# Who multiplies the attention probabilities: VectorE instead of GpSimd in two of four branches

## The reference

```python
ya = banded_chunk_attention(aq, ak, av, 8 previous chunks, rel_bias)    # branch a
yb = mla(...)                                                           # branch b, dense, chunk-causal
yc = banded_chunk_attention(rope(cq), rope(ck), cv, 2 previous chunks, sinks)  # branch c, "local"
ym = memory_attention(mq, mem, w_mem_kv)                                # branch m, 256 memory tokens
gated = concatenate([ya * silu(ag), yb * silu(bg), yc * silu(cg), ym * silu(mg)])
h = layer_norm(alpha * x + gated @ w_out)
```

## Time and profile before

| | us |
|---|---|
| median of three timed runs | 3718.03 (3717.81 to 3725.36) |
| the profiled execution's own time | 3720.31 |
| its span, first to last instruction | 3718.5 |
| busy: TensorE | 3462.1 (93%) |
| busy: GpSimd | 1573.3 (42%) |
| busy: VectorE | 1544.2 (42%) |
| busy: ScalarE | 1002.5 (27%) |

### The profile page before, as it was taken

One profiled execution on the slowest core, in us unless ns is written; L12 is line 12 of the kernel. 1 busy time (PEld: TensorE's weight loads), 2 busy tenths in 40 slices (PEclk: granted clock), 3 DMA queues, 4 the chain that ended last, 5 costly groups with the idle time before them and its releaser, 6 DMA issues.

```text
span 3718.5 us, 50039 instructions
## 1 busy us (share of the span) xinstructions
PE 3462.1 (93%) x20022; PEld 1785.2 (48%) x20340; DVE 1544.2 (42%) x2435; ACT 1002.5 (27%) x1744; POOL 1573.3 (42%) x1034
## 2 busy tenths in 40 slices
PE   7988997998999799999987999999998979999999
PEld 4554653645564344444434554555544434444444
DVE  3255347145436733331115455545554463333100
ACT  1433322233332300000002455554554320000000
POOL 4444652444564233332324555645554423333232
PEclk9999999998999999999999999999999999999999
DMA  3100112110021111111121101111011111111112
GB/s 121 41 19 35 60 60 83 46 33 32 23 85 36 34 51 51 51 51 47 52 72 73 47 28 48 48 46 48 27 48 72 45 34 52 50 51 51 48 48 80
DMA packets 52885, 188.33 MB, mean 51 GB/s; under 512 B 6624, under 2 KB 7136, under 8 KB 52192
## 3 DMA queue, kind: packets, MB, share of 16 engines
q1 hardware_dynamic: 51408, 181.08, 13.9%
q10 hardware_dynamic: 1296, 4.72, 0.3%
HBM read 173.20 MB, written 12.58 MB: 50 GB/s over the span
## 4 chain that ended last, share of the span: by engine, by line
PE 85%; DVE 5%; ACT 5%; issue 3%; POOL 1%; DMA 1%; SPq 0%; DVEq 0%; POOLq 0%; ACTq 0%
PE pair L1028 25%; PE pair L1026 24%; PE pair L1027 21%; PE pair L1238 3%; PE pair L1207 2%; PE pair L1460 2%; PE pair L1219 2%; DVE arena L1884 2%; PE pair L1436 1%; PE pair L1419 1%; ACT arena L1804 1%; POOL panel_parts L825 1%; ACT arena L1636 1%; PE pair L1367 1%; PE pair L1046 1%
## 5 line engine op out<-in xcount | busy, mean ns | idle before, releaser
L1026 PE MATMUL pair<-operand,panel_parts 128*128 128x512 f16 x2816 | 1075.6, 382 | 90.4 <-POOL panel_parts L825 61.3
L1028 PE MATMUL pair<-operand,panel_parts 128*128 128x512 f16 x2816 | 1071.7, 381 | 12.2
L1027 PE MATMUL pair<-operand,panel_parts 128*128 128x512 bf16 x2584 | 984.4, 381 | 0.0
L824 POOL TENSOR_SCALAR panel_parts<-panel_raw 128x1024 f16<-128x1024 f32 (+3 forms) x287 | 296.0, 1031 | 1568.1 <-PE pair L1028 1054.5
L825 POOL TENSOR_TENSOR panel_parts<-panel_raw,panel_parts 128x1024 bf16<-128x1024 f32 (+3 forms) x287 | 633.7, 2208 | 23.9
L1026 PE MATMUL pair<-arena,panel_parts 128*128 128x512 f16 (+1 forms) x1216 | 464.4, 382 | 41.1 <-DVE arena L1884 29.6
L1026 PEld LDWEIGHTS pair<-operand,panel_parts 128*128 128x128 f16 x2816 | 276.0, 98 | 440.1 <-issue 143.2
L859 POOL TENSOR_SCALAR arena<-arena,row_inv 128x256 f32<-128x256 f32 (+7 forms) x256 | 338.6, 1335 | 344.2 <-DVE row_inv L1946 343.9
L1028 PE MATMUL pair<-arena,panel_parts 128*128 128x512 f16 (+1 forms) x1216 | 463.7, 381 | 5.4 <-issue 1.1
L1028 PEld LDWEIGHTS pair<-operand,panel_parts 128*128 128x128 bf16 x2816 | 276.7, 98 | 336.5 <-issue 7.2
L1027 PE MATMUL pair<-arena,panel_parts 128*128 128x512 bf16 (+1 forms) x1130 | 429.8, 380 | 0.0
(11 more groups left out here) (213 smaller groups left out, 4241.4 us busy)
## 6 DMA issues: line engine op xcount, KB each, us to landing
panel_raw<-in_wgu SPq DMA_DIRECT2D x88, 512.0 KB, 3.2
panel_raw<-in_wl SPq DMA_DIRECT2D x58, 512.0 KB, 3.2
panel_raw<-in_wm SPq DMA_DIRECT2D x56, 512.0 KB, 3.3
panel_raw<-in_wdn SPq DMA_DIRECT2D x32, 512.0 KB, 3.2
residual_spill<-residual SPq DMA_DIRECT2D x16, 512.0 KB, 2.9
residual<-residual_spill SPq DMA_DIRECT2D x15, 512.0 KB, 5.9
panel_raw<-in_wl SPq DMA_DIRECT2D x18, 384.0 KB, 2.9
panel_raw<-in_wdn SPq DMA_DIRECT2D x16, 384.0 KB, 2.9
```

The lines of the kernel that those rows point to most:

```text
L824: chained(nc.gpsimd.tensor_scalar(WP[:, s, 0, 0:cols], RAW[:, s, 0:cols], HI_MAX, -HI_MAX, ALU.min, ALU.max))
L1026: nc.tensor.matmul(out, stat[0], mov[0], start=first, stop=False)
L1027: nc.tensor.matmul(out, stat[0], mov[1], start=False, stop=False)
L1028: return nc.tensor.matmul(out, stat[1], mov[0], start=False, stop=last)
```

## The change

For branches c and m, `slot_invert` now also multiplies the probabilities by the inverse row sum, on VectorE, after a wait for its own reciprocal; each multiply raises a new semaphore, `slot_scaled_dve`. GpSimd's `scale` returns at once for these branches. TensorE's transposes wait for the semaphore of the engine that scaled their slot, at counts from a new table, `SCALED_AT`; GpSimd's wait for the reciprocals of branches a and b uses `INVERSE_AT`, which counts those two branches alone. In c and m VectorE's reciprocal no longer raises `slot_inverse`.

```diff
+SCALED_AT, _scaled = {}, {"ab": 0, "cm": 0}
+for _n, (_, _s) in enumerate(SLOTS):
+    _side = "cm" if _s.branch in "cm" else "ab"
+    for _u in [u for g in _s.groups for u in g]:
+        _scaled[_side] += 1
+        SCALED_AT[_n, _u.i] = _scaled[_side]
+INVERSE_AT = [2 * sum(s.branch in "ab" for _, s in SLOTS[:n]) for n in range(len(SLOTS))]
...
             def scale(n, group):
                 _, s = SLOTS[n]
-                pool.wait_ge(slot_inverse, 2 * n + group + 1)
+                if s.branch in "cm":
+                    return
+                pool.wait_ge(slot_inverse, INVERSE_AT[n] + group + 1)
                 for u in s.groups[group]:
...
             def slot_turn(n, g):
 
                 l, s = SLOTS[n]
-                pe.wait_ge(slot_scaled, PROBS_AT[n, s.groups[g][-1].i])
+                pe.wait_ge(slot_scaled_dve if s.branch in "cm" else slot_scaled, SCALED_AT[n, s.groups[g][-1].i])
...
-                V_.reciprocal(RI[:, c], RS[:, c]).then_inc(slot_inverse, 1)
+                if s.branch not in "cm":
+                    V_.reciprocal(RI[:, c], RS[:, c]).then_inc(slot_inverse, 1)
+                    return
+                chained(V_.reciprocal(RI[:, c], RS[:, c]))
+                for u in units:
+                    p = probs_of(n, s, u)
+                    b = 4 * (n % 2) + u.i
+                    V_.tensor_scalar(p, p, RI[:, b:b + 1], None, ALU.mult).then_inc(slot_scaled_dve, 1)
```

More of the change, by code:

```diff
@@ L496, in build @@
         slot_scaled = sem("slot_scaled")
+        slot_scaled_dve = sem("slot_scaled_dve")
         slot_turned = [sem(f"slot_turned{b}") for b in range(2)]
```

## The result

The changed kernel takes 3724.11 us (median of 14 executions, 3718.98 to 3728.70); the kernel before, run beside it, 3718.11 (14 executions, 3713.19 to 3725.36). The ratio is 1.0015, 95% interval 1.0008 to 1.0022: 5.6 us slower, somewhere between 3.0 and 8.2. The interval leaves out no change at all, so the change costs something, and it lies inside the 0.2% called "the same" in the prediction; the median is 0.9 us above its 3723.2.

The account below looks back on a forecast made before the run. TensorE bounds the memory branch, a chain through several engines the local one. Slots add 3 x 0.55 + 0.43 + 0.52 = 2.60 us a layer, 5.2 for two: 3723.2 us on the median 3718.0, range 3717 to 3729.

Parts of the forecast that it names:

- Place: Second multiply pair, between VectorE's reciprocal and copy L1956 (second transposed half), delays TensorE's values; 0.55 us a pair.
- Which slots pay: Local branch, first layer: 18, 19, 22 pay 0.55 us each, 16 pays 0.43, 20 pays 0.52; 17 and 21 pay 0.
- Price: One 128x256 multiply on VectorE takes 0.298 us, 0.22 of VectorE's time; a pair 0.55, at most 0.79, at least 0.29.
- Slot 16: Local branch: VectorE's copy has 0.12 us of slack before TensorE can start the values, so the pair costs 0.43 us.
- Slot 20: Local branch: two pairs cost 1.10 us, four faster 32x1024 copies give back 0.58 (the relief), leaving 0.52 us.
- Memory branch nothing: Memory branch: VectorE waits 0.85 to 1.60 us after its second reciprocal, hiding the pairs; 7.7 us if not.
- The wait at 483.45: Memory stage: TensorE's 1.24 us wait, put down to GpSimd's multiply, is not GpSimd's; no gain counted, otherwise 2.5 us.
- Rival A: Local stage: longer stalls drop TensorE's clock to half; over 0.2% slower, with four falls 12.0 us, 3730.0 us; chance 0.14.
- Rival B: Multiplies at upper price (pair 0.79 us), no relief from slot 20's faster copies: 10.3 us, 3728.3 us; chance 0.07.
- Rival C: Nearly nothing to pay: 483.45's wait was GpSimd's (2.7 us, 3720.7) or lower price (2.1 us, 3720.1); chance 0.13.
- Rival D: VectorE's multiplies meet GpSimd's panel splits, adding at most 3.6 us: 8.8 in all, 3726.8 us; chance 0.05.
- Rival E: Faster by over 0.2%: half-clock stretches vanish as slot 20 gets its copies sooner; needs 12.6 us back; chance 0.03.

Follow-up runs that it names:

- the same work behind the copy: Changed kernel, each second group's multiplies moved behind VectorE's copy of the previous slot's second transposed half; ratio 1.0003 to the kernel before, median 3720.67 us.
- the second pair back on GpSimd: Changed kernel, but GpSimd scales the second group of each local-branch slot again; ratio 1.0002 to the kernel before, median 3720.01 us.
- the memory branch alone: Changed kernel, but VectorE scales only the memory branch and GpSimd keeps the local one; ratio 0.9998 to the kernel before, median 3719.97 us.

## Why the prediction was right

- **Place.** "The new multiplies go exactly between these two": shown by the kernel with the same work behind the copy, and by the second pair back on GpSimd; with either the waits go back to those of before, or 0.11 to 0.12 over.
- **Which slots pay.** 16, 18, 19, 20 and 22, as said; 17 and 21 nothing of their own. The second layer repeats the waits (1.79, 1.32, 1.79).
- **Price.** The term that was mis-sized: 0.298 us a multiply by a line through rows of 512 and 1,024 elements, 0.55 a pair. Measured 0.351 and 0.64. The line's fixed part was too small; its slope was near: 128 and 256 elements differ by 68 ns, 0.53 ns an element. The spacing of two is 0.27 against 0.22. The upper bound of 0.79 held it.
- **Slot 16** paid 0.61 where 0.43 was said; 0.09 of the difference is the price, and the rest a slack of 0.03 where 0.12 was read off: the prediction took the modelled end of TensorE's last product (266.55) for the start of the values, which is at 266.48. **Slot 20** paid 0.60 against 0.52: 1.30 for two pairs, 0.70 back (0.56 by the four copies, 0.15 by the two additions ahead of them, which took 1.56 us beside GpSimd and take 1.41).
- **The sum** by measured terms is 0.61 + 3 x 0.64 + 0.60 = 3.1 a layer, 6.3 us in all, against 5.2 predicted and 5.6 (3.0 to 8.2) by the ratio. The interval can't tell 5.2 from 6.3, so that the median came within 0.9 us of the forecast is luck; the waits, not the time, show that the sum was some 1 us short. The two profiled executions differ by only 3.9 us: in the second layer of the changed kernel's two stretches at half clock are shorter (clock 0.90 in its local stage against 0.86).
- **Memory branch nothing:** right, by the memory branch alone. Not foreseen: on GpSimd the multiplies there can meet VectorE's add and cost 0.33 us a slot, which the change rules out.
- **The wait at 483.45** was not GpSimd's: right.
- **Rival A**, the clock, did not come with stalls of 1.79. With 2.32 it came in slot 22 and not in slot 18, so it was real, but no length of stall by itself decides it in these traces. **Rival B** had the price nearer (0.34 an operation), not the missing relief. **Rival C** fell: a pair costs 0.64, not 0.29, and the wait at 483.45 is still there. **Rival D** did not occur: a multiply takes at most 355 ns, all 128 of them. The rule that the prediction quotes there is narrower in the Trainium skill, "SBUF — State Buffer", § Who interferes with whom: the lock for a whole instruction is stated for VectorE's 2-port modes, not for every single-source operation. **Rival E** fell: the mean clock of the two profiled executions is 0.978 and 0.979, and the changed kernel is slower.

## What to carry to other kernels

Work moved to an engine with idle time costs where it stands ahead of something that the busiest engine waits for: 126 us of busy time taken from GpSimd gave nothing, 0.64 us put in front of one copy cost 0.64 us per slot, and with the same work behind the copy the waits are 0.11 to 0.12 us over those of before. When the trace names one engine as the end of a wait, compare the ends of all the producers with the start of the waiter. And a copy that releases the busiest engine should stand ahead of work for the next step: here moving two such copies gave four times what the change cost.

## What the hardware showed that was not expected

- The time of one and the same kernel follows the mean granted clock: 35 executions of the kernel before went from 3712.86 us at 0.982 to 3727.70 at 0.976. A difference of 0.1% needs many executions, or the waits.
- Idle stretches can cost twice: 0.53 us more in five waits a layer made 5.3 us of waiting, and the time grew by 13 us more, with a lower clock in every execution. The same stall of 2.32 us was followed by half clock in one slot and by full clock in another.
- A VectorE add (128x512, both inputs in SBUF) beside GpSimd multiplies took 0.69 or 1.02 us, with GpSimd 0.56 us longer in the first case, both at the same offset of 2.70 us.
- Two small operations in a row on VectorE overlap: a multiply takes 351 ns, but the next starts 0.27 us behind it.
